# Router products from rows in front of the norm, turns inside the next tile's products, mixed rows packed: one decoder layer on one core

## The reference

```
y            = Mixer(x)                       # x @ w_in, pooling and gated conv, then @ w_out
x1           = LN(alpha*x + y) * ln1_g + ln1_b
g_logits     = x1 @ w_group  + b_group        # 4 groups, top 1
e_logits     = x1 @ w_expert + b_expert       # 32 experts, top 2 in the group
f            = sum over the 2 experts of gate * (silu(x1 @ w1[e]) * (x1 @ w3[e])) @ w2[e]
out          = LN(alpha*x1 + f) * ln2_g + ln2_b
```

## Time and profile before

| | us |
|---|---|
| median of 3 runs (lowest, highest) | 695.56 (692.65, 697.58) |
| the profiled execution | 698.17 |
| its span, first to last instruction | 696.4 |
| busy PE / DVE / ACT / POOL | 598.3 / 307.1 / 217.7 / 160.0 |
| moved by DMA | 236.07 MB |

### The profile page before, as it was taken

How to read it: one execution, slowest core, us unless ns; L and a number is a source line. 1 busy time by engine, 2 the same in 40 slices (tenths; PEclk the granted TensorE clock), 3 DMA queues, 4 the chain that set the end, 5 groups by cost and what they waited for, 6 DMA issues and landing times.

```text
span 696.4 us, 10578 instructions
## 1 busy us (share of the span) xinstructions
PE 598.3 (86%) x4194; PEld 413.3 (59%) x4194; DVE 307.1 (44%) x785; ACT 217.7 (31%) x316; POOL 160.0 (23%) x187
## 2 busy tenths in 40 slices
PE   5999999999999999999999777777788677768783
PEld 5999999977886555555555344444444444445351
DVE  3454286615567415354535243333333433333544
ACT  3242313401122314534453242414323232424040
POOL 1000000000000323344243323332222232233333
PEclk8899999999999999999999999999999999999998
DMA  9990330746199999999999999999999999999991
GB/s 248 259 336 18 135 121 1 300 186 271 61 360 423 329 415 417 416 417 419 421 417 414 416 417 420 421 420 422 421 420 420 419 419 418 421 418 418 420 405 64
DMA packets 45786, 236.07 MB, mean 339 GB/s; under 512 B 13700, under 2 KB 18308, under 8 KB 28888
## 3 DMA queue, kind: packets, MB, share of 16 engines
q1 hardware_dynamic: 32191, 220.92, 78.8%
q0 software_dynamic: 12688, 11.78, 5.1%
q10 hardware_dynamic: 857, 2.67, 1.0%
HBM read 238.22 MB, written 30.20 MB: 385 GB/s over the span
## 4 chain that ended last, share of the span: by engine, by line
PE 43%; DMA 33%; SPq 16%; DVE 5%; issue 1%; ACT 1%; POOL 0%; POOLq 0%; DVEq 0%; ACTq 0%
DMA blocks<-in_w 24%; PE ps L548 14%; PE ps L723 11%; SPq L401 10%; PE ps L605 7%; DMA eleventh_block<-in_w 7%; PE ps L744 6%; SPq L405 4%; DMA blocks<-in_w_in 1%; PE ps L634 1%; PE ps L709 1%; PE ps L732 1%; PE ps L618 1%; SPq L425 1%; DVE blocks L1283 1%
## 5 line engine op out<-in xcount | busy, mean ns | idle before, releaser
L723 PE MATMUL ps<-blocks,ln 128*64 128x256 f32 x1952 | 224.8, 383 | 45.6 <-DMA blocks<-in_w 44.1
L723 PEld LDWEIGHTS ps<-blocks,ln 128*64 128x64 f32 x1952 | 151.6, 138 | 120.2 <-issue 67.9
L744 PE MATMUL ps<-blocks,hT 128*64 128x512 f32 x480 | 111.0, 604 | 22.1 <-DMA blocks<-in_w 21.3
L744 PEld LDWEIGHTS ps<-blocks,hT 128*64 128x64 f32 x480 | 32.8, 138 | 82.0 <-issue 52.8
L1018 ACT ACTIVATE std<-rstd,eps 128x1 f32<-128x1 f32 x32 | 9.4, 294 | 211.6 <-DVEq L1570 211.5
L1538 DVE SCALAR_TENSOR_TENSOR h_rows<-silu,slot_gate,ps 128x256 f32<-128x256 f32 x33 | 15.8, 480 | 97.2 <-PE ps L723 97.0
L1126 POOL DMA_INDIRECT out<-prev,final_row x32 | 32.1, 1002 | 86.8 <-DVE prev L1576 85.9
L1122 POOL DMA_INDIRECT prev<-first_outputs,final_row x32 | 34.0, 1062 | 77.6 <-DMA first_outputs<-ye,first_row 46.7
L548 PE MATMUL ps<-xT_high,w_in_high 128*128 128x288 f32 x256 | 42.3, 309 | 4.7 <-ACT w_in_high L827 3.5
L968 ACT ACT_TABLE_LOAD x30 | 38.5, 1283 | 20.8 <-PE ps L723 20.4
L1549 DVE TENSOR_TENSOR ye<-ye,ps 128x512 f32<-128x512 f32 x16 | 11.0, 688 | 71.8 <-PE ps L744 71.8
(11 more groups left out here) (242 smaller groups left out, 765.6 us busy)
## 6 DMA issues: line engine op xcount, KB each, us to landing
blocks<-in_w SPq DMA_DIRECT2D x86, 2048.0 KB, 43.2
eleventh_block<-in_w SPq DMA_DIRECT2D x8, 2048.0 KB, 44.8
blocks<-in_w_in SPq DMA_DIRECT2D x3, 2048.0 KB, 10.0
blocks<-in_w_out SPq DMA_DIRECT2D x2, 2048.0 KB, 7.8
blocks<-in_w SPq DMA_DIRECT2D x4, 1024.0 KB, 37.6
x_tok<-in_x_prompt SPq DMA_DIRECT2D x4, 512.0 KB, 5.4
blocks<-in_w_in SPq DMA_DIRECT2D x4, 512.0 KB, 11.9
first_outputs<-in_x_prompt SPq DMA_DIRECT2D x4, 512.0 KB, 8.3
```

The lines of the kernel that those rows point to most:

```text
L723: mm = pe.matmul(ps[64 * g:64 * g + 64, bank, 0:FH], x, w[:, k, g * FH:(g + 1) * FH], start=(k == 0), stop=(k == KD - 1))
L744: mm = pe.matmul(ps[64 * g:64 * g + 64, BY, :], hT[:, k % 2, k // 2 * SLOTS:(k // 2 + 1) * SLOTS], w[:, k, g * DH:(g + 1) * DH], start=(k ...
```

## The change

Five things:

- **Order of norm and router.** The norm is x1 = (z - mean) * rstd * g + b with z = alpha*x + y. The router's weights are multiplied by g once, early; `route` multiplies rows z themselves; `keep_logits` then makes (z @ (g*W) - mean * sum(g*W)) * rstd + (bias + b @ W). The two column sums come from one product with ones, between `project(8)` and `project(9)`. So `turn_x1(j, h)` waits only for the residual of half h, and DVE's rows are normed (`normalise`) after they are turned.
- **Where PE turns.** Tile j-1 is turned inside `out_project(1, j)`, four transposes in front of k = 2 and four in front of k = 3; the first half of the last tile in front of k = 6 of `out_project(1, 4)`. `x1T` has two copies. Between `out_project(1, 4)` and `route(4)` stand `route(3)`, four transposes and four warming products.
- **Last tile.** Its norm is three instructions on POOL (64 rows x 1024), after `rows_scaled`; `fetch_first` waits for them too, and the last store of x1 follows them. On ACT the square root of the last tile and the store of tile 3 come behind the last `keep_x1T`.
- **Warming products.** 15 in a row behind `route(4)` become 6 groups of 3, each released by three more steps of DVE's chain.
- **Memory.** Seven eighths of `mix_high` lie in block 4, the last eighth beside `mix_low`. Block 3 is free after `in_done` 16, and `load(3)` is issued there.

```diff
+        mix_high = at("mix_high", BLOCKS_AT + 4 * 4 * BLK, KD - 1, T, dt=F32R)
+        mix_high_last = at("mix_high_last", MIX_AT + 4 * KD * T, T, dt=F32R)
...
-            sp.dma_start(w_router[:, :, 0:EG], w_group.rearrange("(p k) c -> p k c", k=KD)).then_inc(router_loaded, 16)
-            sp.dma_start(w_router[:, :, EG:NR], w_expert.rearrange("(p k) c -> p k c", k=KD)).then_inc(router_loaded, 16)
+            for h in range(2):
+                half = slice(h * DH, (h + 1) * DH)
+                for w, c in ((w_group, slice(0, EG)), (w_expert, slice(EG, NR))):
+                    sp.dma_start(w_router[:, h * KH:(h + 1) * KH, c],
+                                 w[half, :].rearrange("(q i) c -> q i c", i=KH)).then_inc(router_loaded, 16)
+                for a, x in enumerate((ln1_g, ln1_b)):
+                    sp.dma_start(ln1_cols[:, a, h * KH:(h + 1) * KH],
+                                 x[half].rearrange("(q i) -> q i", i=KH)).then_inc(router_loaded, 16)
...
             load(1)
             load(2)
+            load(3)
...
             sp.wait_ge(out_done, 2 * NT)
             load(0)
-            load(3)
             load(4)
             load(8)
...
+            for c in range(6, 9):
+                project(c)
+            pe.wait_ge(router_scaled, 1)
+            pe.wait_ge(ones_made, 1)
+            pe.wait_ge(map_kept, NG)
+            pe.matmul(ps[:, 7, 0:2 * NR], ones_wide, router_sums, start=True, stop=True).then_inc(router_summed, 1)
+            for c in range(9, 13):
                 project(c)
...
-            def turn_x1(j):
+            def turn_x1(j, h):
                 r = ROWS[j]
-                pe.wait_ge(x1_ready, j + 1)
+                pe.wait_ge(out_kept, h * NT + j + 1)
                 if j:
-                    pe.wait_ge(x1T_ready, 2 * j)
+                    pe.wait_ge(x1T_ready, 2 * j + h - 1)
...
-            out_project(1, 1)
-            turn_x1(0)
-            for j in range(2, NT):
-                out_project(1, j)
-                route(j - 2)
-                turn_x1(j - 1)
+            for j in range(1, NT):
+                turns = [(2, lambda: turn_x1(j - 1, 0)), (3, lambda: turn_x1(j - 1, 1))]
+                if j == NT - 1:
+                    turns.append((6, lambda: turn_x1(j, 0)))
+                out_project(1, j, turns)
+                route(j - 1)
+            turn_x1(NT - 1, 1)
             pe.wait_ge(out_kept, NT + 3)
             keep_warm(4)
-            route(NT - 2)
-            turn_x1(NT - 1)
-            keep_warm(2)
             route(NT - 1)
-            keep_warm(15)
+            for i in range(1, 7):
+                pe.wait_ge(step, ROUTE_STEP + 3 * i)
+                keep_warm(3)
...
             def fetch_first():
                 pe.wait_ge(hot_ready, 1)
+                pe.wait_ge(x1_ready, NT)
...
+            for j in range(NT - 1):
+                deviation(j)
                 keep_x1T(j)
+                if j:
+                    store_x1(j - 1)
+            keep_x1T(NT - 1)
+            deviation(NT - 1)
+            store_x1(NT - 2)
+            store_x1(NT - 1)
...
+            r, row = ROWS[NT - 1], x_tok[0:ROWS[NT - 1], NT - 1, :]
+            pool.wait_ge(rows_scaled, 1)
+            pool.wait_ge(x1_turned, 2 * NT)
+            g.tensor_scalar(row, row, mv1[0:r, NT - 1, 0:1], rstd[0:r, NT - 1, 0:1],
+                            ALU.subtract, ALU.mult).then_inc(rows_centred, 1)
+            pool.wait_ge(rows_centred, 1)
+            g.tensor_tensor(row, row, ln1[0:r, 0, :], ALU.mult).then_inc(rows_centred, 1)
+            pool.wait_ge(rows_centred, 2)
+            g.tensor_tensor(row, row, ln1[0:r, 1, :], ALU.add).then_inc(x1_ready, 1)
...
+            settled(v.tensor_tensor(router_b, w_router, b_cols, ALU.mult))
+            settled(v.tensor_reduce(router_sums[:, NR:2 * NR], router_b.rearrange("p k c -> p c k"), AX.X, ALU.add))
+            settled(v.tensor_tensor(w_router, w_router, g_cols, ALU.mult))
+            v.tensor_reduce(router_sums[:, 0:NR], w_router.rearrange("p k c -> p c k"), AX.X,
+                            ALU.add).then_inc(router_scaled, 1)
...
             for j in range(NT):
-                residual(0, j).then_inc(out_kept, 1)
+                settled(residual(0, j))
+                dve.sem_inc(out_kept, 1)
+                v.bn_stats(stats1[0:ROWS[j], j, 0:6], x_tok[0:ROWS[j], j, 0:DH])
...
+            for j in range(NT - 1):
+                measure(j)
+                scale_of(j)
+                if j:
+                    keep_logits(j - 1)
+                normalise(j)
+            measure(NT - 1)
+            keep_logits(NT - 2)
+            scale_of(NT - 1)
+            dve.sem_inc(rows_scaled, 1)
+            keep_logits(NT - 1)
```

More of the change, by code:

```diff
@@ L44 @@
 PAIRS = E // 2
+ROUTE_STEP = 74
 EARLY_BLOCKS = 10
@@ L162, in build @@
         ln1 = sb("ln1", [P, 2, D])
+        x1T_more = nc.alloc_sbuf_tensor_at("x1T_more", [P, 4 * P], F32, offset=small[0])[:, :]
         h_rows = sb("h_rows", [P, FH])[:, :]
@@ L230, in build @@
         counts = equal_flat[:, 0:HIST]
+        here = x1T_at + 8 * P - 5 * D - 3 * D // 4
+        router_sums = equal_flat[:, here:here + 2 * NR]
+        here += 2 * NR
+        ln1_cols = equal_flat[:, here:here + 2 * KD].rearrange("p (a k) -> p a k", a=2)
+        here += 2 * KD
+        stats1 = equal_flat[:, here:here + 12 * NT].rearrange("p (j s) -> p j s", j=NT)
+        here += 12 * NT
+        mv1 = equal_flat[:, here:here + 2 * NT].rearrange("p (j s) -> p j s", j=NT)
+        ones_wide = ye_flat[:, 0:P]
+        router_b = ye_flat[:, P:P + KD * NR].rearrange("p (k c) -> p k c", k=KD)
         xe = ln1[:, 0, :].rearrange("p (g d) -> p g d", g=2)
@@ L590, in _, with out_project @@
                 project(c)
-            def out_project(h, j):
+            def out_project(h, j, between=()):
                 o = h * NT + j
@@ L603, in out_project @@
                         pe.wait_ge(mix_is_low, k + 1)
+                    for at_k, turn in between:
+                        if at_k == k:
+                            turn()
                     for i, (a, b) in enumerate(((0, 0), (0, 1), (1, 0))):
-                        mm = pe.matmul(ps[0:r, o % 4, :], mix_part[a][:, k, j * P:j * P + r],
+                        mm = pe.matmul(ps[0:r, o % 4, :], mix_part(a, k)[:, j * P:j * P + r],
                                        wout_part[h][b][:, k, :], start=(i == 0 and k == 0),
@@ L1106, in _ @@
                               v[:, PV:VEXT].rearrange("p (b t) -> p b t", b=NB)[:, :, NS:]).then_inc(vtail_kept, 1)
+            pool.wait_ge(map_done, NG)
+            g.memset(ones_wide, 1.0).then_inc(ones_made, 1)
             for c in range(NG):
@@ L1228, in _ @@
             steps = [0]
-            deviations = [0]
             def settled(ins):
@@ L1308, in _ @@
                 low_of_w(c)
+            dve.wait_ge(router_loaded, 160)
+            dve.wait_ge(map_done, NG)
+            g_cols, b_cols = [ln1_cols[:, a, :].unsqueeze(2).to_broadcast([P, KD, NR]) for a in range(2)]
+            settled(v.tensor_tensor(router_b, w_router, b_cols, ALU.mult))
[3 more added lines that the diff above has]
+                            ALU.add).then_inc(router_scaled, 1)
             for c in range(NG):
@@ L1353, in residual, with measure @@
                 return v.scalar_tensor_tensor(x, x, ALPHA, ps[0:r, o % 4, :], ALU.mult, ALU.add)
[L1355 to L1362, removed]
-                deviations[0] += 1
-                dve.wait_ge(std_ready, deviations[0])
-                settled(v.reciprocal(scale, std[0:r, :]))
-            def norm1(j):
+            def measure(j):
                 r = ROWS[j]
@@ L1371, in norm1, with scale_of, normalise @@
                 dve.sem_inc(out_kept, 1)
+                settled(v.bn_stats(stats1[0:r, j, 6:12], x_tok[0:r, j, DH:D]))
+                settled(v.bn_aggr(mv1[0:r, j, :], stats1[0:r, j, :]))
+                dve.sem_inc(var_ready, 1)
+            def scale_of(j):
+                dve.wait_ge(std_ready, j + 1)
+                settled(v.reciprocal(rstd[0:ROWS[j], j, 0:1], std[0:ROWS[j], :]))
+            def normalise(j):
+                r = ROWS[j]
                 row = x_tok[0:r, j, :]
-                deviation_of(row, r)
-                v.scalar_tensor_tensor(row, row, mv[0:r, 0:1], ln1[0:r, 0, :], ALU.subtract, ALU.mult)
-                scale_of(r, rstd[0:r, j, 0:1])
+                dve.wait_ge(x1_turned, 2 * j + 2)
+                settled(v.scalar_tensor_tensor(row, row, mv1[0:r, j, 0:1], ln1[0:r, 0, :], ALU.subtract, ALU.mult))
                 v.scalar_tensor_tensor(row, row, rstd[0:r, j, 0:1], ln1[0:r, 1, :], ALU.mult,
```

72 lines of the change are left out of this document (36 added, 36 removed).

## The result

The changed kernel takes 699.90 us (median of 6 runs, 698.11 to 701.20) where the kernel before takes 695.59 (6 runs): ratio 1.0066, interval 1.0037 to 1.0094. It is 4.3 us slower in the one and 3.0 in the other. I had forecast 1.1 us faster, 694.5, in a range up to 699.8. Both differences are within the 1% that I gave 0.90.

The account below looks back on a forecast made before the run. The weight stream's start bounds it, through queued bytes and PE's and DVE's chain. Gain between 0.6 us (last store) and 1.5 (chain), taken as 1.1: 695.56 - 1.1 = 694.5 us, chance 0.44, range 690.3 to 699.8.

Parts of the forecast that it names:

- What bounds the kernel: Weight stream at about 420 GB/s, rate unchanged; its start is limited by queued bytes and PE's and DVE's chain together.
- second part: From the last residual (E) to the issue of load 10; 21.43 us before, 17.1 by the prediction's own sum.
- first part: From the residual of tile 0's second half to the last residual (E); 28.67 us before, forecast 31.35 plus 0.2.
- Turns inside the products: PE's transposes inside second-half output products, stalls put at zero; last residual (E) comes 2.9 us later, at 194.7.
- rival B: Turns overlap the products and the stream alone decides: 4.3 us earlier by PE's chain, 691.3 us; chance 0.07.
- E to the logits: From the last residual (E) to the last logits: about 5.1 us in place of 9.4, chain starting 1.4 to 1.5 earlier.
- Chain to `fetched`: DVE and PE work from last logits to `fetched`, awaited by load 10: unchanged 12.0 us, so `fetched` 1.5 earlier, at 211.8.
- rival A: POOL's two-input instructions hold DVE's chain of small steps 4.4 us: `fetched` 2.9 late, 698.5 us; chance 0.33.
- rival C: Warming groups put mask products back 1.5 us at low clock, or turns wait 0.4 each: 695.8 us; chance 0.12.
- Size of the GpSimd instructions: Last tile's norm on POOL: three instructions of 2.2 us, 6.6 in all, with nobody waiting for the rows.
- Last store: Last store of x1 lands by about 213.5 and releases load 10, 1.7 us behind `fetched`; this limit gives 0.6 us.
- Load 3 early: Load 3 moves to the partly idle ninth slice: 5.0 us of stream go there, leaving three blocks before load 10.

Follow-up runs that it names:

- e10: Kernel before with three extra GpSimd instructions (multiply, tensor_scalar, multiply, each 64 x 512) into unused memory from the last logits on; ratio 1.0016 to the kernel before.
- e2: Changed kernel with only GpSimd's first norm instruction kept, gain and bias of the last 64 rows left out; 692.0 us, ratio 0.9979 to the kernel before.
- second measurement: Changed kernel again, unmodified, on another chip: 697.55 us against 694.55 for the kernel before, ratio 1.0044.
- e1: Changed kernel with the last tile's norm on VectorE instead of GpSimd; 693.3 us against 694.3 for the kernel before, ratio 0.9994.
- e7: Changed kernel with the last tile's norm on VectorE, split so its first instruction precedes the scale; 691.9 us against 694.3 for the kernel before, ratio 0.9972.
- e3: Changed kernel with the 15 warming products in one row again instead of six groups; ratio 1.0054 to the kernel before.
- e5: Changed kernel with the last tile's norm on VectorE and the 15 warming products in one row; ratio 1.0016 to the kernel before.
- e6: Changed kernel with the last tile's norm on VectorE and load 3 back behind the last output product; ratio 1.0014 to the kernel before.
- e8: e7 with two warming products in place of four ahead of the last route; ratio 0.9997 to the kernel before.
- e9: Kernel before with load 3 early alone (and `x1T` moved 64 elements further on); ratio 0.9991 to the kernel before.

## Why the prediction was wrong, by its steps

- **What bounds the kernel**: right. The stream runs at 420 GB/s in both, and the time follows its start. Every ratio above 1.004 has a second part above 22 with the longer first part. The second part alone does not set the time: e10 has the longest, 25.03, with four blocks queued and the old first part, and 1.0016.
- **Turns inside the products**: first part 31.83, forecast 31.35 (the 0.2 for the product with ones lies ahead of it and does not belong in this sum). Each period is 8.25 where I had 8.15, and the last half turn costs 0.7 where I had 0.5; no wait inside the products. Right, and rival B, in which the turns cost nothing, falls.
- **E to the logits**: 5.0, forecast 5.1. Right; with the first part 3.2 longer, the chain starts 1.2 us earlier, about as forecast (1.4).
- **Chain to `fetched`, "Unchanged: 201.25 to 213.29, 12.0 us"**: this is the term of the sum that failed. From the last logits to load 10 the changed kernel took 217.56 - 199.01 = 18.55 us. In e2, without GpSimd's two-input instructions, it took 12.2. Two sentences of the prediction put the cost at nothing, "The narrow stretch is now half as long, so I take no loss" and "At 2.2 nobody waits for the rows". I costed GpSimd's norm as work beside other work. Its length was hidden, though only just (the rows were ready at E + 11.9, and the fetch began at E + 12.0 in e2, at E + 18.4 in the changed kernel), but two of its instructions held VectorE's chain for 4.3 us. I had this as rival A, with 4.4 us, and gave it less chance than no holding at all, on one short row. Then the groups of warming products, which I had tied to the steps' pace, turned the holding into 2.1 us more, through the clock; I had kept 1.5 as the bound of that. Rival A and rival C are not two cases but one chain; together they are 6.4 us, where A alone was 4.4. That the time passed my upper end, by 0.1 us, says little: the end, 699.8, was A's 698.5 plus 1.3 (not plus 1, as the prediction says), and the second measurement's ratio puts the kernel at 698.7, inside it. What is shown is the sign and the cause.
- **Size of the GpSimd instructions**: 3.79, 2.33, 2.34, where I took 2.2 each. The one-input instruction with two operations was the longest.
- **Last store**: landed at 213.8, forecast 213.5. Right, and hidden behind `fetched`, so it set nothing, where the forecast had it release load 10. In e1 and e7, with `fetched` at E + 18, it no longer mattered either, since the store was issued earlier.
- **Load 3 early**: "5.0 us of the stream", of which the dry queue takes back most. In the changed kernel the engines stood still some 5 us more than before in the 52 us from E + 2 on (the sum of one less the DMA share over half-microsecond stretches: 5.3 and 0.2). So the account of the slow-down, an estimate from these sums, is: first part +3.2, idle engines +5.1, load 3 -5.0, 3.3 us; measured 4.3 and 3.0. The same account gives e1 -1.1 (measured -0.4), e2 -1.6 (-1.5), e3 +2.7 (+3.7), e5 -0.3 (+1.1), e6 +2.3 (+1.0), e7 -1.5 (-1.9), e8 -0.8 (-0.2), e9 -2.0 (-0.6), e10 +2.2 (+1.1): right to about 1.4 us, which no run here resolves further. Whether the early load 3 gains anything by itself thus stays open; e6 and e9 both point to a gain, and neither shows it.
- The Trainium skill ("SBUF — State Buffer", section "Who interferes with whom") says that a VectorE instruction with two SBUF inputs contends with a GpSimd instruction that reads SBUF. That rule gave the better forecast than my reading. The trace agrees with it for two-input instructions on both sides (2.35 us held, 0.2 without). In e2 and in the changed kernel it does not show it where GpSimd's instruction reads one tensor: 3.79 us of it beside two-input steps of 0.18. There the measurement decides: this instruction did not hold VectorE for its length. One such step in e10 took 0.25 us more, which stays open.

## What to carry to other kernels

Work that is moved to an idle engine is free only if it holds up nothing on the critical one. Here each two-input GpSimd instruction that ran beside a chain of short VectorE steps held one two-input step until it ended, 2.35 us in place of 0.2. The norm on VectorE itself took 2.6 us, of which 1.15 reached the logits; on GpSimd its two two-input instructions took 4.7 us and cost 6.4. Warming products that are tied to another engine's steps follow its stalls and can then be the last to end: in these traces the groups gained 1.1 us over a plain row where the steps kept their pace, and lost 1.1 where they were held. When two rivals share their trigger, add their prices and do not spread them over two cases.

## What was not expected of the hardware

GpSimd's tensor_scalar with two pointer scalars took 3.79 us for 64 x 1024 and 2.08 for 64 x 512, longer than its two-input multiply (2.33 and 1.28). It was the shorter one that held VectorE's two-input steps for its whole length, and the longer one that did not. The granted clock is on an edge in this stretch: with two warming products less, about 0.45 us of PE's work, it was 0.50 in place of 1.00 from 196 to 202 (e8 and e7, one profiled execution of each).
